# The opening of a two-block kernel: order of the first weight pieces, and the root mean square of x by pairs of row tiles

## What is computed

```python
def rmsnorm(x, g):
    xf = x.astype(jnp.float32)
    y = xf * lax.rsqrt(jnp.mean(xf * xf, axis=-1, keepdims=True) + EPS)
    return (y * g.astype(jnp.float32)).astype(x.dtype)

def modulate(h, shift, scale):
    return h * (1 + scale) + shift
...
        mod_l = (jax.nn.silu(c) @ ada_w[l] + ada_b[l]).reshape(b, ADA_CHUNKS, 1, D_MODEL)
        mod_c = (jax.nn.silu(c_ctx) @ ada_w[l] + ada_b[l]).reshape(ADA_CHUNKS, D_MODEL)
        h_l = modulate(rmsnorm(x, norm1_g[l]), mod_l[:, 0], mod_l[:, 1])
        h_c = modulate(rmsnorm(xc, norm1_g[l]), mod_c[0], mod_c[1])
...
    z_c = h_c @ w_in
    z_l = h_l @ w_in
```

## Time and profile before

| | us |
|---|---|
| median of 3 runs | 2415.34 |
| lowest and highest | 2413.61, 2419.32 |
| span of the profiled execution | 2414.8 |
| TensorE busy in it | 2282.1 (95%) |
| VectorE busy | 1410.9 (58%) |
| ScalarE busy | 491.5 (20%) |

### The profile page before, as it was taken

One profiled execution on the slowest core, in us unless ns is written; L12 is line 12 of the kernel. 1 busy time (PEld: TensorE's weight loads), 2 busy tenths in 40 slices (PEclk: granted clock), 3 DMA queues, 4 the chain that ended last, 5 costly groups with the idle time before them and its releaser, 6 DMA issues.

```text
span 2414.8 us, 29902 instructions
## 1 busy us (share of the span) xinstructions
PE 2282.1 (95%) x11586; PEld 1589.0 (66%) x11586; DVE 1410.9 (58%) x2731; ACT 491.5 (20%) x1064; POOL 203.6 (8%) x392
## 2 busy tenths in 40 slices
PE   7999889999999976999999999989999999988998
PEld 3445555864686434499588865658867876656875
DVE  2136754586676258277557742468758765247775
ACT  2122532311131135222011101321101101132110
POOL 1000001305523420000010000000000000000000
PEclk9999999999999987999999999899999999999999
DMA  8546402324434538444565455145455544514542
GB/s 287 204 154 235 146 18 79 99 88 157 158 131 151 189 106 337 151 140 162 187 206 164 146 164 176 53 133 170 147 178 177 173 145 153 172 35 157 175 147 97
DMA packets 253580, 371.18 MB, mean 154 GB/s; under 512 B 24838, under 2 KB 182144, under 8 KB 248704
## 3 DMA queue, kind: packets, MB, share of 16 engines
q1 hardware_dynamic: 235952, 332.36, 41.8%
q0 software_dynamic: 16624, 36.31, 4.7%
q10 hardware_dynamic: 864, 0.59, 0.1%
HBM read 345.10 MB, written 22.02 MB: 152 GB/s over the span
## 4 chain that ended last, share of the span: by engine, by line
PE 83%; DVE 11%; ACT 2%; issue 1%; DMA 1%; SPq 1%; DVEq 0%; ACTq 0%
PE banks L224 74%; DMA weights<-in_w_in 1%; PE banks L3220 1%; PE banks L1770 1%; PE banks L458 1%; DVE big L3308 1%; PE banks L3832 1%; SPq L2636 1%; PE banks L3818 1%; DVE big L1135 1%; PE banks L2501 1%; PE banks L2983 0%; PE banks L1448 0%; PE banks L1804 0%; DVE normed_rows L2071 0%
## 5 line engine op out<-in xcount | busy, mean ns | idle before, releaser
L224 PE MATMUL banks<-weights,big 128*128 128x256 f32 (+4 forms) x2128 | 578.3, 441 | 10.9 <-issue 7.9
L224 PE MATMUL banks<-weights,h_columns 128*128 128x256 f32 (+4 forms) x1664 | 536.8, 478 | 12.3 <-issue 4.6
L224 PEld LDWEIGHTS banks<-weights,big 128*128 128x128 f32 (+2 forms) x2128 | 338.7, 185 | 202.9 <-issue 142.1
L224 PEld LDWEIGHTS banks<-weights,h_columns 128*128 128x128 f32 x1664 | 317.0, 192 | 209.7 <-issue 151.8
L224 PE MATMUL banks<-big 128*128 128x256 f32 x1040 | 235.5, 383 | 14.2 <-DVE big L3295 8.2
L224 PEld LDWEIGHTS banks<-big 128*128 128x128 f32 x1040 | 199.5, 192 | 43.7 <-issue 8.9
L3342 DVE TENSOR_TENSOR big<-banks,big 128x256 f32<-128x256 f32 x308 | 130.1, 422 | 89.8 <-PE banks L224 84.5
L224 PE MATMUL banks<-h_columns,weights 128*128 128x128 f32 (+1 forms) x896 | 147.1, 320 | 6.1 <-ACTq L3008 1.8
L224 PE MATMUL banks<-normed_rows,big 128*128 128x384 f32 (+2 forms) x480 | 142.0, 440 | 2.9 <-issue 2.1
L224 PEld LDWEIGHTS banks<-h_columns,weights 128*128 128x128 f32 x896 | 129.9, 191 | 16.8 <-DVEq L3008 2.0
L2571 POOL DMA_DIRECT2D s_inside<-kernel_lags x256 | 127.4, 506 | 40.9 <-ACT statistics L2555 38.6
(11 more groups left out here) (528 smaller groups left out, 2610.7 us busy)
## 6 DMA issues: line engine op xcount, KB each, us to landing
weights<-in_mlp_w SPq DMA_DIRECT2D x52, 1024.0 KB, 5.5
weights<-in_ada_w SPq DMA_DIRECT2D x48, 1024.0 KB, 7.9
weights<-in_ffn_w_gate SPq DMA_DIRECT2D x44, 1024.0 KB, 5.1
weights<-in_ffn_w_up SPq DMA_DIRECT2D x44, 1024.0 KB, 5.1
weights<-in_ffn_w_down SPq DMA_DIRECT2D x48, 768.0 KB, 4.3
weights<-in_w_out SPq DMA_DIRECT2D x12, 1024.0 KB, 6.2
weights<-in_mlp_w SPq DMA_DIRECT2D x16, 768.0 KB, 4.3
weights<-in_w_in SPq DMA_DIRECT2D x16, 768.0 KB, 4.4
```

Source lines behind the costliest of these rows:

```text
L224: ins = T.engine.matmul(out, lhsT, rhs, start=start, stop=stop)
```

## The change

1. **The list.** The two pieces of unit 1 move from before the first piece of `w_in` to behind it. The fifth piece is now the projection's; unit 1's are the sixth and seventh.
2. **TensorE.** Unit 2's products move between the transposes of row tiles 0 and 1 and those of 2 and 3. Unit 1's products move from ahead of the projection to behind t = 0, unit 3's products to behind t = 1 with unit 1's turn, unit 3's turn to behind t = 2, right ahead of the second transposes. `weights_used` is raised by 4 behind t = 3.
3. **POOL.** It issues x without the wait for the first piece. Two row tiles share a semaphore.
4. **The root by pairs.** ScalarE waits for a pair, squares it, and takes the root; VectorE scales the first tile of the pair, ScalarE the second, each with a semaphore of its own, on which the transposes wait.

```diff
@@ -353,11 +353,10 @@
             at += k
         e.dma_start(self.raw[0:96, 1, :], a["ada_b"].rearrange("l (k n) -> (l k) n", n=P))\
             .then_inc(self.sem("constants_loaded"), 16)
-        e.wait_ge(self.sem("slot0_loaded"), 16)
         for t in range(TT):
             src = a["x"] if t < TL else a["ctx"]
             r = (t % TL) * P
-            e.dma_start(self.x[:, t, :], src[0, r:r + P, :]).then_inc(self.sem(f"x{t}_loaded"), 16)
+            e.dma_start(self.x[:, t, :], src[0, r:r + P, :]).then_inc(self.sem(f"x{t // 2}_loaded"), 16)
         for j, name in enumerate(("ret_lg_f", "ret_lg_b")):
             e.dma_start(self.lgr[:, 0, j * H:(j + 1) * H], a[name].to_broadcast([P, H]))\
                 .then_inc(self.sem("tables_loaded"), 16)
@@ -530,20 +529,21 @@
         self.tensor_ada_products(T, rows0)
         self.tensor_vectors(T)
         self.tensor_ada_turn(T, n0, bank0, rows0, buffer0)
-        self.tensor_ada_products(T, rows2)
-        self.tensor_turn_half(T, 0)
+        self.tensor_turn_half(T, 0, lambda: self.tensor_ada_products(T, rows2))
         self.tensor_ada_turn(T, n2, bank2, rows2, buffer2)
         for k in range(4):
             T.hand([k], self.by_parity(k))
-        self.tensor_ada_products(T, 4)
-
-    def tensor_turn_half(self, T, half):
+
+    def tensor_turn_half(self, T, half, between=None):
 
         for k in range(4 * half, 4 * half + 4):
             T.engine.wait_ge(*T.freed(k))
         for t in range(TT):
+            if t == TL and between:
+                between()
             if half == 0:
-                T.engine.wait_ge(self.sem("rows_ready"), T.due("rows_ready"))
+                rows = "open_rows_from_" + self.by_parity(t)
+                T.engine.wait_ge(self.sem(rows), T.due(rows))
             for k in range(4 * half, 4 * half + 4):
                 ins = T.engine.transpose(self.ps[:, k, t * P:(t + 1) * P], self.xnr[:, t, k * P:(k + 1) * P],
                                          self.ident[:, :])
@@ -551,10 +551,10 @@
 
     def tensor_between(self, T, t):
 
-        if t == 0:
-            self.tensor_ada_products(T, 5, beside=True)
         if t < 2:
-            n, rows, bank, buffer = self.OPEN_UNITS[2 + t]
+            self.tensor_ada_products(T, self.OPEN_UNITS[2 + t][1], beside=True)
+        if t in (1, 2):
+            n, rows, bank, buffer = self.OPEN_UNITS[1 + t]
             self.tensor_ada_turn(T, n, bank, rows, buffer)
         if t == 2:
             self.tensor_turn_half(T, 1)
@@ -598,17 +598,26 @@
         V.engine.wait_ge(self.sem("open_scales"), V.due("open_scales", 2))
 
     def vector_open_rms(self, V):
-        for t in range(TT):
-            V.engine.wait_ge(self.sem(f"x{t}_loaded"), V.due(f"x{t}_loaded", 16))
-        self.vector_rms(V, range(TT))
+        for t in range(0, TT, 2):
+            V.engine.wait_ge(self.sem("squares_ready"), V.due("squares_ready"))
+            self.vector_rsqrt(V, self.sm[:, 32 + t:34 + t], self.sm[:, 16 + t:18 + t], 1.0 / D, EPS)
+            V.engine.sem_inc(self.sem("open_roots"), 1)
+            V.engine.tensor_scalar(self.xnr[:, t, :], self.x[:, t, :], self.sm[:, 32 + t:33 + t], None, ALU.mult)\
+                .then_inc(self.sem("open_rows_from_vector"), 1)
+        V.engine.wait_ge(self.sem("open_rows_from_vector"), V.due("open_rows_from_vector", 2))
 
     def scalar_open_rms(self, A):
-        for t in range(TT):
-            A.engine.wait_ge(self.sem(f"x{t}_loaded"), A.due(f"x{t}_loaded", 16))
-            ins = A.engine.activation(self.xnr[:, t, :], self.x[:, t, :], ACT.Square, accum_out=self.sm[:, 16 + t:17 + t])
-        ins.then_inc(self.sem("squares_ready"), 1)
-        A.engine.wait_ge(self.sem("squares_ready"), A.due("squares_ready"))
-        self.scalar_root(A, self.sm[:, 32:32 + TT])
+        for pair in range(0, TT, 2):
+            A.engine.wait_ge(self.sem(f"x{pair // 2}_loaded"), A.due(f"x{pair // 2}_loaded", 32))
+            for t in (pair, pair + 1):
+                ins = A.engine.activation(self.xnr[:, t, :], self.x[:, t, :], ACT.Square, accum_out=self.sm[:, 16 + t:17 + t])
+            ins.then_inc(self.sem("squares_ready"), 1)
+            A.engine.wait_ge(self.sem("squares_ready"), A.due("squares_ready"))
+            self.scalar_root(A, self.sm[:, 32 + pair:34 + pair])
+            A.engine.wait_ge(self.sem("open_roots"), A.due("open_roots"))
+            A.engine.activation(self.xnr[:, t, :], self.x[:, t, :], ACT.Copy, scale=self.sm[:, 32 + t:33 + t])\
+                .then_inc(self.sem("open_rows_from_scalar"), 1)
+        A.engine.wait_ge(self.sem("open_rows_from_scalar"), A.due("open_rows_from_scalar", 2))
 
     def scalar_open(self, A):
         for half in range(2):
...
@@ -1361,6 +1361,7 @@
                 src = a["w_in"][0][part * 512:(part + 1) * 512, s:s + width].rearrange("(k p) n -> p k n", p=P)
                 self.slots.append((src, P, 4 * width))
                 if s + part == 0:
+                    self.list_ada(0, 1)
                     self.list_ada(0, 3)
                 elif n < 12:
                     self.list_ada(0, n)
@@ -1411,7 +1412,7 @@
             elif s == 0:
                 self.tensor_between(T, t)
                 if t == TT - 1:
-                    ins.then_inc(self.sem("weights_used"), 2)
+                    ins.then_inc(self.sem("weights_used"), 4)
             if what == "turn":
                 self.tensor_lora_turn(T, i)
             elif what == "q":
@@ -4183,7 +4184,7 @@
 
     with ExitStack() as ctx:
         K = Kernel(nc, ctx, a)
-        for n in (0, 2, 1):
+        for n in (0, 2):
             K.list_ada(0, n)
         K.list_mixer1()
         K.list_mlp0()
```

More of the change, by code:

```diff
@@ L684, in scalar_root @@
         A.engine.wait_ge(self.sem("root_done"), A.due("root_done"))
[L686 to L693, removed]
     def norm_parts(self):
```

## The result

The change takes 2420.83 us in the median of 16 runs (2414.02 to 2425.08), the kernel before beside it 2415.18 (16 runs, 2409.0 to 2420.18). The ratio is 1.0018 [1.0009, 1.0026], which is +4.3 us [2.2, 6.3]: slower, by less than the 0.2% bound of 4.8 us. By the ratio, on the forecast's own base of 2415.34, the change takes 2419.7: kind and range held, both by less than 1 us, and the size was too small. The median itself, 2420.83, lies 0.3 above the range. The profiled execution took 2417.78 us, its span is 2415.9.

The account below looks back on a forecast made before the run. TensorE, busy 2282.1 of 2414.8 us, was taken as the bound, only its waits in the opening being winnable. -0.85 + 1.92 + 0.45 = +1.5 us gave 2416.8 us by the median; range 2412.5 to 2420.5, its own 2415.5 to 2418.1.

Parts of the forecast that it names:

- x asked for at once: POOL's issue of x: at 4.45 instead of 7.53 us, 3.1 us sooner, pushing weights behind x without adding bandwidth.
- The fourth piece: Weight DMA, second half of unit 2: lands at 23.5 us in place of 21.38, 2.1 us later.
- The way from there to the start: TensorE from the fourth piece through products, transposes, turn and modulation: projection starts at 31.0 us, 0.85 sooner than 31.83.
- Unit 1's products behind the start: TensorE, between the first and second row tile: 16 products formerly in the DMA's shadow, +1.92 us.
- The new wait: TensorE, before the second transposes: they need the bank of the turn right ahead freed, +0.45 us (bounds 0.27 and 0.8).
- VectorE's gamma work: VectorE, behind unit 1's rows: over by 43.7 us, before unit 3's rows at 43.9, so hidden, and barely.
- The weight stream: Weight DMA near the half's end: three pieces land by 67.6 us, the third wanted at 68.60; 0 in the sum.
- The clock at the start: First eight projection passes: the low clock's 1.7 us (5.37 in place of 3.68) stays as before, so 0.
- High clock at the fourth piece: Rival, TensorE's opening: earlier activity brings the high clock before 23.5 us; +0.2 us, 2415.5 us; chance 0.13.
- The hole not coming again: Rival, opening DMA: the 2.2 us pause behind x belongs to the moment; -0.7 us, 2414.6 us; chance 0.12.
- The start following the projection piece: Rival, projection start: fourth piece not pushed back, TensorE begins near 28 us; 2412.2 us, or 2410.4 at 26.2; chance 0.06.
- Slower, the low clock into the first tile: Rival, TensorE's opening: clock low until the second row tile, 4.9 us on top, 2421.7 us; chance 0.12.

Follow-up runs that it names:

- the new stream: Kernel before with only the change's weight list, TensorE's order of the later units and the raise by 4; no timed ratio, fourth row tile at 52.41 us.
- second profile: The kernel before, unedited, profiled once more for the scatter of its marks: 2415.44 us in one execution, first tile 3.67 us.
- x held: Against the change: POOL again waits for the first weight piece before asking for x; ratio to before 1.0003 [0.9992, 1.0014], median 2418.57 us.
- the gains later: Against the change: the two gain loads issued only behind the first half of h; ratio to before 1.0011 [0.9999, 1.0024], median 2420.25 us.

## Why the forecast was right in kind and short in size

That kind and range held was in part luck. The forecast's own range, worked out from its mechanism, ended at 2418.1, +2.8 us, and the +4.3 lies beyond it, in what the wider range adds. Of the step on which the change rested, the sooner start, not even the sign came true.

- *x asked for at once*: right. Issued at 4.42 (forecast 4.45); it only moved bytes. Pair 0's row began at 17.35, pair 1's at 21.44, each done in 1.15: 18.5 and 22.6 (forecast 18.6 and 22.9). They wait for the fourth piece, as said. The second piece's slip, an estimate of 1.3 without its working, was 1.19 (11.50 against 10.31).
- *The fourth piece*, 23.5 forecast, 24.66 to 25.21 measured: **the step that failed first.** The count of bytes was right (4.57 MB at 23.5). What it left out is that a piece is complete with the slowest engine's share, and that x asked for at once, with the small tables behind it, spreads the shares: 2.28 us in place of 1.09, about the +1.16 that was missing.
- *The way from there to the start*: products at the low clock as forecast, 1.86 from start to start. The transposes took 1.77 (forecast 1.5), the turn about 1.7 (1.05), from its end to the start 3.02 (2.94). With the piece: +1.16 - 0.08 + 0.27 + 0.66 + 0.08 = 2.1, which is 33.01 against 30.9 (the prediction's terms add to 30.93, which it wrote as 31.0). "Transposes half and half, turn high" was the second failed choice: in before the clock was high behind eight products and eight transposes in a row; in the change the eighth transpose is the last, so by that row all eight should have been put low. The turn behind them was low as well in two of three profiles (1.71), high in the other (0.95). So the term -0.85 became +1.18.
- *Unit 1's products behind the start*, +1.92: 1.86. Right. *The new wait*, +0.45: 0.42 of idleness, and the turn, no longer overlapped by passes, 0.15 more. Right.
- *VectorE's gamma work* "hidden, and barely": not quite hidden. The copy of unit 3's rows began at 46.11, behind ScalarE's last gamma step, while the products ended at 45.9; TensorE didn't wait for it. *The weight stream*, 0: right, the row at 70.70 has no wait.
- *The clock at the start*, 0: 5.58 against 5.37 in the two profiles compared, so right by these. But the row of before on which it stood was no typical one. Over all profiles, in the kernels with before's list TensorE idled 1.2 to 1.9 us ahead of the first tile and the tile took 3.67 in five of six; in those with the new stream it idled 3.0 us and the tile took 5.05 to 6.49 in eight of eight. Against an execution of before with a fast first tile, such as its second profile, this term is 1.4 to 1.9 us in the change, not 0. Whether the longer idleness is the reason isn't shown: no run changed it alone.
- *The rivals.* High clock at the fourth piece: in one of three executions of the change, and gone again with the transposes. The Trainium skill (TensorE: Matmul & The Clock Gate, What's actually happening) says that activity releases the throttled state. The trace agrees only in part: in the change with x held or the gains later, where TensorE went into the fourth piece's products after 0 to 0.52 us of waiting, they ran at the high clock in three of four profiles; after waits of 2.47 to 2.81, in one of three. So few profiles show no rule. The hole not coming again: it came; it belongs to the gain loads, as the rows' order had said. The start following the projection piece: the fourth piece came at 24.66, not before 21.5. Slower, the low clock into the first tile: in part; transposes and turn paid 0.9 of its 1.25, but the tile took 5.58, not 7.1, and the 16 products 1.92, not 3.8. The range took in two rivals, not three: 2412.2 lies under its lower end of 2412.5.

In sum -0.85 + 1.92 + 0.45 = +1.5 became +1.18 + 2.78 = +3.96: the gain at the start, on which the change rested, turned into a loss.

## What to carry to other kernels

Asking for data sooner gives no bandwidth: count which critical piece is pushed behind it, and add that a piece is complete only with its slowest engine's share, which here came some 1.2 us later when x and the tables moved beside it. Look for the small loads that hold the DMA engines, and see which piece stands behind them; here moving two loads of 48 KB brought the fourth tile of before 2.1 us sooner, where the whole change brought it 3.9 later. Work that fills an idle stretch ahead of the main loop isn't free to move: it goes behind the start at full price, and the longer idleness may cost clock as well.

## What the runs showed of the hardware

- Two loads that spread one small row over 128 partitions, 48 KB each, took the transfer rate from 365 to 124 GB/s for 2.5 us in the change, and from 354 to 150 for 3.5 us in the kernel before. Moved in the change, they passed at 33 to 35 us, where the rate was 242 GB/s and not 386. In the kernel before, the 16 packets of the second load, 3072 bytes each, took 1.21 to 2.16 us, those of the first 0.16 to 0.18.
- The 16 shares of one weight piece of 1 MiB landed 0.76 to 1.16 us apart where x came behind the first piece, and 1.88 to 2.87 apart where x was asked for at once; the piece counts only with the last.
- The total scatters by where the clock falls, far from any edit. The same work of the change, from about 137 us to the 5531st matmul near 1070 us, took 929.3, 938.4 and 929.5 us in its three profiles; the granted clock was 0.50 for 58.0, 78.5 and 58.0 us of it. In the first profile of before it took 932.1, with 68.3 us at 0.50, so that 2.8 of the 3.96 us came back there. So spans of the change ran from 2412.6 to 2424.9, more than the whole effect: a single execution tells nothing of 4 us here, the marks in the opening do.
- The profile's clock column seems to lack records: in the first profile of the change it reads 1.00 from 25 to 33 us, where eight transposes took 1.97 and the turn 1.71, as in the third profile at 0.50; with x held or the gains later the transposes took 1.09 to 1.10. Here the durations decide.
